# Splitting each matmul of the mixers' out product into a block of 192 tokens and a block of 64

## What is computed

```python
for l in range(DEPTH):                                   # DEPTH = 2
    xn = rmsnorm(x, norm_mix[l])
    proj = xn @ w_in[l]
    ...                                                  # five mixers, 256 channels each
    cat = jnp.stack([y_pool, y_conv, y_diff, y_sc, y_mem], axis=2)
    cat = rmsnorm(cat, group_norm[l].reshape(N_GROUPS, GROUP_WIDTH)).reshape(b, s, MIX_WIDTH)
    x = x + cat @ w_out[l]                               # 256 x 1280 times 1280 x 1024
    x = x + peer_ffn(rmsnorm(x, norm_ffn[l]), peer_wq[l], peer_subkeys[l], peer_u[l], peer_v[l])
```

## Time and profile before

| | before |
|---|---|
| median of 3 runs | 3560.04 us (3558.72 to 3570.94) |
| the profiled execution, its own time | 3564.15 us |
| its span, first to last instruction | 3562.8 us |
| mean granted TensorE clock | 0.944 of 2.4 GHz |
| busy PE / PEld / DVE / ACT / POOL | 3245.5 / 2768.5 / 2063.8 / 1664.8 / 221.6 us |
| DMA | 479.91 MB, 135 GB/s on average |

### The profile page before, as it was taken

The page is one execution under the profiler, slowest core; times in us unless marked ns, Lnnn a source line. Parts: engine busy times, 40 slices in busy tenths (PEclk is TensorE's granted clock), DMA queues, the critical chain, the costliest instruction groups (busy, mean ns, idle before and its releaser), DMA issues.

```text
span 3562.8 us, 51089 instructions
## 1 busy us (share of the span) xinstructions
PE 3245.5 (91%) x19360; PEld 2768.5 (78%) x19360; DVE 2063.8 (58%) x4132; ACT 1664.8 (47%) x3572; POOL 221.6 (6%) x290
## 2 busy tenths in 40 slices
PE   7998999998899777996899999987699779999999
PEld 4745677786699766985689999987598658999998
DVE  2233433335665665598666666656558876666665
ACT  2244322223654335419755555543451685555554
POOL 0021000000200160000000000006100000000000
PEclk9999899997999787999999999978699999999999
DMA  5402344432156322440355555543053115655554
GB/s 207 177 1 83 128 174 166 151 109 72 48 181 179 108 78 65 149 160 1 105 185 185 187 185 188 185 137 106 12 178 131 65 36 184 189 184 184 189 185 153
DMA packets 135059, 479.91 MB, mean 135 GB/s; under 512 B 15520, under 2 KB 17440, under 8 KB 134048
## 3 DMA queue, kind: packets, MB, share of 16 engines
q1 hardware_dynamic: 132944, 471.26, 40.6%
q10 hardware_dynamic: 1872, 5.38, 0.4%
HBM read 475.53 MB, written 1.05 MB: 134 GB/s over the span
## 4 chain that ended last, share of the span: by engine, by line
PE 84%; DVE 8%; issue 4%; ACT 3%; DMA 1%; SPq 0%; ACTq 0%; DVEq 0%
PE psum L706 14%; PE psum L708 14%; PE psum L707 14%; PE psum L2370 7%; PE psum L2371 7%; PE psum L2372 7%; PE psum L2292 6%; PE psum L2216 4%; PE psum L557 3%; PE psum L999 2%; PE psum L354 1%; PE psum L571 1%; DVE conv_part L1457 1%; DVE w_lo L248 1%; PE psum L1009 1%
## 5 line engine op out<-in xcount | busy, mean ns | idle before, releaser
L248 DVE TENSOR_TENSOR w_lo<-raw,w_hi 128x512 fp32r<-128x512 f32 x1472 | 1005.9, 699 | 821.1 <-ACT w_hi L239 793.7
L239 ACT ACTIVATE w_hi<-raw 128x512 fp32r<-128x512 f32 x1472 | 894.8, 625 | 882.3 <-PE psum L708 495.8
L706 PE MATMUL psum<-x_hi,w_hi 128*128 128x256 f32 x2096 | 604.8, 289 | 30.7 <-DVE w_lo L248 23.4
L707 PE MATMUL psum<-x_lo,w_hi 128*128 128x256 f32 x2096 | 600.6, 287 | 0.0
L708 PE MATMUL psum<-x_hi,w_lo 128*128 128x256 f32 x2096 | 597.2, 285 | 0.0
L706 PEld LDWEIGHTS psum<-x_hi,w_hi 128*128 128x128 f32 x2096 | 401.9, 192 | 43.6 <-DVE w_lo L248 25.7
L2370 PE MATMUL psum<-w_hi,wt_hi 128*128 128x512 f32 x1024 | 407.3, 398 | 6.5 <-DVE wt_lo L2428 6.5
L707 PEld LDWEIGHTS psum<-x_lo,w_hi 128*128 128x128 f32 x2096 | 404.0, 193 | 8.2
L2371 PE MATMUL psum<-w_lo,wt_hi 128*128 128x512 f32 x1024 | 407.0, 397 | 0.0
L2372 PE MATMUL psum<-w_hi,wt_lo 128*128 128x512 f32 x1024 | 407.0, 397 | 0.0
L708 PEld LDWEIGHTS psum<-x_hi,w_lo 128*128 128x128 f32 x2096 | 406.8, 194 | 0.0
(11 more groups left out here) (315 smaller groups left out, 4652.4 us busy)
## 6 DMA issues: line engine op xcount, KB each, us to landing
raw<-in_v SPq DMA_DIRECT2D x256, 512.0 KB, 4.2
raw<-in_u SPq DMA_DIRECT2D x190, 512.0 KB, 3.4
raw<-in_mod_w SPq DMA_DIRECT2D x96, 512.0 KB, 4.2
raw<-in_w_gate_up SPq DMA_DIRECT2D x88, 512.0 KB, 4.8
u_raw<-in_u SPq DMA_DIRECT2D x66, 512.0 KB, 3.5
raw<-in_w_in SPq DMA_DIRECT2D x40, 512.0 KB, 4.0
raw<-in_w_down SPq DMA_DIRECT2D x32, 512.0 KB, 3.6
raw<-in_w_peer SPq DMA_DIRECT2D x32, 512.0 KB, 4.2
```

The costliest lines, as they stand in the source:

```text
L239: self.nc.scalar.activation(self.hi[:, m % 4, :], self.half(m), ACT.Copy).then_inc(self.rounded[m % 4], 1)
L248: self.nc.vector.tensor_tensor(self.lo[:, m % 4, :], self.half(m), self.hi[:, m % 4, :], ALU.subtract).then_inc(self.ready[m % 4], 1)
L706: pe.matmul(out[:, 0:width], hi[:, w], x_hi, start=(c == 0), stop=False)
L707: pe.matmul(out[:, 0:width], hi[:, w], x_lo, start=False, stop=False)
```

## The change

`Residual` takes a list of token blocks, and where it has one it calls a new `product_by_tokens` in place of `product`. The mixers' out products get the blocks 0 to 192 and 192 to 256. The order of chunks and of the three parts stays; each of the three matmuls becomes two, one over the first 192 columns of the same bank and rows and one over the last 64, with the same stationary block. The first matmul of a tile alone carries the start mark. `Ring.free` is called with the last matmul of a half, now one of 64 columns. Nothing else differs.

```diff
+def product_by_tokens(k, out, cuts, x, blocks):
+
+    pe = k.nc.tensor
+    c, total = 0, sum(cuts)
+    for part in halves(cuts):
+        hi, lo = k.ring.take()
+        for j in range(part):
+            w = slice(j * P, (j + 1) * P)
+            x_hi, x_lo = x(c)
+            for n, (weights, rows) in enumerate(((hi, x_hi), (hi, x_lo), (lo, x_hi))):
+                for a, b in blocks:
+                    mm = pe.matmul(out[:, a:b], weights[:, w], rows[:, a:b], start=(c == 0 and n == 0 and a == 0),
+                                   stop=(c == total - 1 and n == 2), skip_group_check=True)
+            c += 1
+        k.ring.free(mm)
...
 class Residual:
...
-            product(k, use.tensor, self.cuts, self.x, self.width)
+            if self.blocks is None:
+                product(k, use.tensor, self.cuts, self.x, self.width)
+            else:
+                product_by_tokens(k, use.tensor, self.cuts, self.x, self.blocks)
...
         self.out = Residual(k, io[f"w_out{l}"], [5, 5], lambda c: (y_hi[:, c, :], y_lo[:, c, :]), LAT, CTX, None,
-                            self.groups.done)
+                            self.groups.done, blocks=((0, 192), (192, LAT)))
```

More of the change, by code:

```diff
@@ L793, with __init__ @@
 class Residual:
-    def __init__(self, k, w, cuts, x, width, lo, gain, arrive, mods=(), between=None):
-        self.between = between
+    def __init__(self, k, w, cuts, x, width, lo, gain, arrive, mods=(), between=None, blocks=None):
+        self.between, self.blocks = between, blocks
         self.k, self.w, self.cuts, self.x, self.width, self.lo, self.gain = k, w, cuts, x, width, lo, gain
```

## The result

| | before | after |
|---|---|---|
| median | 3563.93 us (5 runs) | 3699.08 us (5 runs) |
| ratio | | 1.038, 95% interval 1.0362 to 1.0399 |

The change made the kernel 135 us slower, against 53 forecast, and the range of 3600 to 3634 us missed it. One of the five executions of the changed kernel took 6329.39 us and is left out of the ratio: in its profile TensorE's records go at about half their pace in untouched stages too (0.22 us from start to start with 256 columns), while the granted clock shown is 1.00.

What follows compares the result with a forecast made beforehand. TensorE's record pace was taken to bound both out products; +26.45 and +26.44 us, together +52.9, on the profiled 3564.15 us gave 3617.1, and 4.1 lower for the median, 3612.9 us, range 3600 to 3634.

Steps and rivals of the forecast that it cites:

- What bounds the kernel: Both out products go at the pace of TensorE's own records; nothing beside them hides a longer stream.
- What sets 0.120 us: Step asking whether 256 moving columns (0.107 us) or the 128-column stationary load sets the out products' record pace.
- the floor: Least time of any record with its own 128-column load: 0.112 us, or 0.212 at the half clock.
- The pace h: Mean time per split record in the out products at full clock: 0.115 us, bounds 0.107 to 0.129.
- The excess I put on the 192-column record: Out products: three quarters of the 0.008 us between 0.112 and 0.120 added, giving 0.118 us for that record.
- the time under that clock brings the same number of records, each worth half as much: Half-clock spans of 5.74 and 3.27 us in the two products stay, holding 27 and 15 records.
- Rival D: Clock stays at 1.2 GHz through both out products: 102.2 us each, +142.8 us, 3703 us; chance 0.04.
- the gates: Evidence against a low clock: 17 records of 128 columns raised it, 496 kept it at 1.00.
- A: Out products: a block's second load is cheap, mean 0.077 us a record, +16.4 us, 3576 us; chance 0.07.
- B: Out products: columns alone set the pace, 0.120 us a pair, time stays 3560 us; chance 0.03.
- The formula from the Trainium skill: N/2.4 + 2.5 ns per matmul: 111.7 ns a pair against 109.2 for 256 columns, 1.2 us for all splits.
- C: Out products: short float32r goes at float32's pace, 3632.6 us, or 3765 if also run as two records; chance 0.06.

Runs made afterwards that it cites:

- e9: Changed kernel plus 12 throwaway plain float32 matmuls of constants, 256 columns wide, ahead of each out product; 3609.98 us, ratio 1.0133 to the kernel before.
- e6: Changed kernel with overlapping blocks 0 to 192 and 64 to 256, two records of 192 columns per matmul; 3613.14 us, ratio 1.0151 to the kernel before.
- e3: Changed kernel with each out-product matmul done twice over all 256 columns instead of split; 3608.94 us, ratio 1.0131 to the kernel before.
- e4: Changed kernel with the first two of 8 tiles of each out product left whole, the other six split; 3598.84 us, ratio 1.0111 to the kernel before.
- e10: Changed kernel with only the first tile of each out product left whole; 3600.29 us, ratio 1.0106 to the kernel before.
- e1: The changed kernel as it stands, measured again in a second session; 3702.57 us, ratio 1.0393 to the kernel before.
- e2: Changed kernel with blocks of 128 and 128 tokens in place of 192 and 64; 3699.98 us, ratio 1.0383 to the kernel before.
- e7: Changed kernel with overlapping blocks 0 to 160 and 96 to 256, two records of 160 columns per matmul; 3700.35 us, ratio 1.0396 to the kernel before.
- e8: Changed kernel with blocks of 128 and 128 and both operands read as plain float32, two records per matmul; 3704.68 us, ratio 1.0399 to the kernel before.

## Why the prediction was wrong

**What bounds the kernel: right.** PE is busy for all of both products and waits for nobody; the other engines only got more slack, and what the rest of the kernel gave back was 2.9 us (143.1 less 140.2).

**What sets 0.120 us: the floor is right.** At the half clock all of 192 + 64, 128 + 128 and 160 + 160 go at 0.213 us a record, whatever the columns. At the full clock 192 and 64 go at 0.112. That it is the load which sets this floor, and not some other cost of each record, remains an inference: every record of these products brings a load of 128 columns, and no run made the load smaller or left it out. The length of the load records does not set the pace: the transposes' loads last 140 ns, and yet four of them in 0.63 us, less 0.27 for one record, stand 0.12 us apart at a clock of 1.00 (L900, from 1273.13 us in the kernel before).

**The pace h at the full clock: 0.115 forecast, 0.112 measured** (e9). The excess I put on the 192-column record is not there; two records of 192 columns (e6) go at 50.21/451 = 0.111 too. With 0.112 my own sum gives +50.1.

**The step that failed** is the sentence "the time under that clock brings the same number of records, each worth half as much": it carried the 5.74 and 3.27 us at the half clock over from the kernel before, as a span of time that the change leaves alone. They are not given. The clock rises because of what TensorE does in them, and the change altered exactly that. With whole matmuls it rose after 3.2 to 6.1 us (e3, e4, e10 and before), with every matmul as a float32r pair of 256 or 320 columns not within 102 (e1, e2 and e7, two products each). The term was 9.0 us of half clock, and measured 204.8. The forecast gave the two products 57.84 + 56.75 = 114.6 us in all and they took 204.8, 90 more, where the whole forecast missed by 86. With one whole tile ahead (e10) the kernel takes 3600.29 us, and with the clock up beforehand (e9) 3609.98, 3 from the forecast: once the clock rises, the rest of the sum is about right.

**Rival D had the right price and a chance of 0.04.** The evidence against it was the gates, and there I read a record of 128 columns of plain float32 as a record of 128 columns. The rows that stood beside it said otherwise: plain float32 needs 0.216 us for 256 columns where float32r needs 0.120, so by that estimate a 128-column record of the gates keeps the array streaming as long as a whole float32r matmul of the product does. Nor were the gates less busy when it counted: I compared 4.04 busy of 6.82 us with a split product that is "busier", but the idle time lay ahead of them, and from their first start 16 records followed one another without a gap, with the clock rising 4.3 us after it:

```profile
1611.52 3.75 PE L2216 MATMUL psum<-hT,first 128*128 128x128 f32 x16 [2.94 <-DVE first L2237]
```

And a row in hand said that a busy PE alone does not raise the clock: 61 records of one column, busy for 12.93 of 12.93 us, stood at 0.50 throughout. e8 beside e2 shows what the type does to this: same width, other type, and the clock rises. The second half of the evidence, that the gates kept a clock of 1.00, was sound but answers another question; the split keeps it as well (e4, e9, e10).

**The other rivals.** A and B are out: the pair costs 0.222 us at the full clock, where they needed 0.154 and 0.120. The formula from the Trainium skill (TensorE: Matmul & The Clock Gate, Back-to-back issue gap), by which a pair would take an estimated 111.7 ns, does not give this stream; the section itself says that it allows nothing for the load and counts too little where the columns are few. The same page's LDWEIGHTS section gives P/1.2 ns for P stationary columns, an estimated 107 ns for 128. The 112 ns a record come near it at the full clock, while at the half clock the rows show 213. C is out in both forms: float32r with 64 and 192 columns went at the floor (e4, e6, e9).

That the clock follows the time in which the array streams is my reading of e2, e3, e6, e7 and e8. It fits all of them, but no row shows the streaming itself. e8 changes the type and doubles the records together with the streaming, so it does not part these; e6 beside e7 parts the columns alone. Why what keeps the clock up does not raise it was not tried.

## What to carry to other kernels

A stretch at the lower TensorE clock is not a constant of a place in the program: before carrying it over, ask whether the changed stream still does what made the clock rise. Splitting matmuls that already go close to the floor of a record (0.120 against 0.112 us here) nearly doubles their time even at the full clock. Where the stream starts at the lower clock it can double once more, by never leaving it; a tile of whole matmuls at the head, or filler in the wait ahead, took that part back here. A busy share does not tell how much the array streams, and columns of different types are not the same columns.

## What was unexpected of the hardware

- The clock has a memory in this kernel: 192 + 64 columns a pair ran 53.7 us at 1.00 when it was up before (e9) and 102.4 us at 0.50 when it was not (e1). The same instructions, 48.7 us apart for each product.
- Streaming more made a kernel faster: 192 + 192 columns a pair took 3613.14 us, and 160 + 160 took 3700.35.
- Twice as many records of plain float32 (e8, 3704.68 us) took about as long as the float32r ones (e2, 3699.98 us), because they raised the clock and the others did not.
